# First shift and scale by halves of their columns, and four tiles of h contracted as soon as they are made

## What is computed

```python
mod = (jax.nn.silu(c) @ w_ada[i] + b_ada[i])[:, None, :]
shift_m, scale_m, gate_m, shift_f, scale_f, gate_f = jnp.split(mod, N_MOD, axis=-1)
h = rmsnorm(x, norm_mix_w[i]) * (1.0 + scale_m) + shift_m
x = x + gate_m * hybrid_mixer(h, w_in[i], ...)
...
proj = h @ w_in
z, xbc, dt_raw, u_pool, gate_logits = jnp.split(proj, IN_SPLITS, axis=-1)
xbc = jax.nn.silu(causal_depthwise_conv(xbc, conv_w, conv_b))
dt = jax.nn.softplus(dt_raw + dt_bias)
```

## Time and profile before

| | |
|---|---|
| time, median of 3 runs | 1705.75 us (1704.42 to 1709.04) |
| the profiled execution's own time | 1708.7 us |
| its span in the trace | 1706.9 us |
| PE busy | 1643.2 us, 96% of the span |
| chain that ended last | PE 80%, DVE 10%, ACT 4% |

### The profile page before, as it was taken

One profiled execution on the slowest core, in us unless ns is written; L12 is line 12 of the kernel. 1 busy time (PEld: TensorE's weight loads), 2 busy tenths in 40 slices (PEclk: granted clock), 3 DMA queues, 4 the chain that ended last, 5 costly groups with the idle time before them and its releaser, 6 DMA issues.

```text
span 1706.9 us, 21913 instructions
## 1 busy us (share of the span) xinstructions
PE 1643.2 (96%) x8026; PEld 1368.7 (80%) x8026; DVE 870.9 (51%) x1222; ACT 682.6 (40%) x1103; POOL 814.4 (48%) x670
## 2 busy tenths in 40 slices
PE   5988999999999999999999999989999999999997
PEld 5776888888878888888888889778878888888886
DVE  6546564656386435644335633677356655013324
ACT  3544445444323322543114322365646544234431
POOL 1373655636445554454444453432255454444443
PEclk7999999999999999999999999999999999999999
DMA  8121221222225445244545542121103142232221
GB/s 318 74 75 50 75 74 74 75 75 99 75 74 198 172 148 204 105 148 161 197 173 180 190 173 99 54 74 68 58 26 124 64 146 96 102 116 90 87 100 65
DMA packets 36825, 194.40 MB, mean 114 GB/s; under 512 B 4080, under 2 KB 6384, under 8 KB 21488
## 3 DMA queue, kind: packets, MB, share of 16 engines
q1 hardware_dynamic: 25200, 151.06, 24.4%
q10 hardware_dynamic: 11520, 41.95, 7.3%
HBM read 190.90 MB, written 2.10 MB: 113 GB/s over the span
## 4 chain that ended last, share of the span: by engine, by line
PE 80%; DVE 10%; ACT 4%; issue 2%; POOL 1%; DMA 1%; DVEq 0%; ACTq 0%; SPq 0%; POOLq 0%
PE main L900 59%; PE main L896 7%; PE main L893 2%; PE auxD L1211 2%; DVE tmp L2010 2%; ACT w_hi L1435 1%; PE main L1000 1%; DVE ada_first L2178 1%; DMA x<-x_in 1%; PE auxD L1276 1%; DVE ysum L2280 1%; PE auxC L1204 1%; PE auxB L1198 1%; DVE tmp L2575 1%; POOL w_lo L720 0%
## 5 line engine op out<-in xcount | busy, mean ns | idle before, releaser
L720 POOL TENSOR_TENSOR w_lo<-raw,w_hi 128x512 fp32r<-128x512 f32 x521 | 693.1, 1362 | 714.4 <-ACT w_hi L1435 710.8
L900 PE MATMUL main<-h_hi,w_hi 128*128 128x512 f32 (+1 forms) x1016 | 399.8, 394 | 1.0 <-DVEq L2077 1.0
L900 PE MATMUL main<-h_hi,w_lo 128*128 128x512 f32 (+1 forms) x1016 | 396.5, 390 | 0.0
L900 PE MATMUL main<-h_lo,w_hi 128*128 128x512 f32 (+1 forms) x1016 | 396.4, 390 | 0.0
L1435 ACT ACTIVATE w_hi<-raw 128x1024 fp32r<-128x1024 f32 (+2 forms) x267 | 258.2, 1015 | 249.1 <-PE main L900 175.2
L900 PEld LDWEIGHTS main<-h_hi,w_hi 128*128 128x128 f32 (+1 forms) x1016 | 190.9, 188 | 41.6 <-issue 2.1
L900 PEld LDWEIGHTS main<-h_hi,w_lo 128*128 128x128 f32 (+1 forms) x1016 | 190.7, 188 | 41.1
L900 PEld LDWEIGHTS main<-h_lo,w_hi 128*128 128x128 f32 (+1 forms) x1016 | 190.8, 188 | 39.4
L2153 DVE SCALAR_TENSOR_TENSOR tmp<-main,par,tmp 128x511 f32<-128x511 f32 x88 | 65.9, 749 | 161.8 <-ACT tmp L1547 160.0
L2178 DVE SCALAR_TENSOR_TENSOR ada_acc<-ada_raw,cs,ada_acc 128x1024 f32<-128x1024 f32 x70 | 106.3, 1519 | 35.0 <-DMA ada_raw<-w_ada 25.5
L2010 DVE SCALAR_TENSOR_TENSOR tmp<-main,half,tmp 128x511 f32<-128x511 f32 (+2 forms) x96 | 71.8, 748 | 44.5 <-ACT tmp L1456 42.1
(11 more groups left out here) (526 smaller groups left out, 2866.7 us busy)
## 6 DMA issues: line engine op xcount, KB each, us to landing
raw<-stream SPq DMA_DIRECT2D x118, 1024.0 KB, 4.8
ada_raw<-w_ada ACTq DMA_DIRECT2D x80, 512.0 KB, 4.5
ada_first<-w_ada SPq DMA_DIRECT2D x16, 512.0 KB, 10.2
raw<-stream SPq DMA_DIRECT2D x8, 768.0 KB, 4.2
raw<-stream SPq DMA_DIRECT2D x8, 640.0 KB, 3.9
x<-x_in SPq DMA_DIRECT2D x4, 512.0 KB, 8.2
x<-x_in SPq DMA_DIRECT2D x1, 2048.0 KB, 9.0
out<-x SPq DMA_DIRECT2D x16, 128.0 KB, 1.8
```

Source lines behind the costliest of these rows:

```text
L720: nc.gpsimd.tensor_tensor(lo[:, a:b], raw[:, s, a:b], hi[:, a:b], ALU.subtract).then_inc(lo_done, 1)
L900: ins = nc.tensor.matmul(bank[0:n, :], w[:, k, col:col + n], a[:, ka_, :], start=start, stop=stop)
```

## The change

- SP brings w_ada by halves of the columns, shift and scale in one DMA: 8 pieces of [128, 2, 512] for columns 0 to 511, then the raw weights of X0 and X1, then 8 pieces for columns 512 to 1023.
- The squares of x go to 8 buffers of their own and PE sums them over tiles and partitions (32 products with one column); DVE's adds go.
- ACT copies the spread 1/root to SBUF, POOL multiplies x by it (tiles 0 to 5 before X0's low pieces, 6 and 7 behind X1's). ACT makes the tile of h from it in two passes: scale and shift into `tmp`, then the rounded copy `h_hi`. `h_lo` becomes a plain subtraction on DVE.
- For the first half, PE takes 5 of the 16 products of w_ada pieces with silu(c) from DVE (`BY_PE`), 4 products with one column each.
- PE contracts DT, X0 and X1 together, over tiles 0 to 3 of h when these are there, then sums the second half of shift and scale, then contracts tiles 4 to 7. DT goes to bank A, so the four main banks hold X0's and X1's tiles, and later jobs are numbered one lower.
- X0 and X1 end together; their convolutions use buffers of their own (`conv_acc`), the tanh of one stands behind the scaling of the next, and `dt_gates`, `dt_sums` and group 0's `xs_turn` move to later slots.

The core of the diff:

```diff
@@ -122,7 +122,7 @@
+        job += 0 if x.name == "DT" else x.n_jobs
@@ -225,12 +225,13 @@
-    mid[find("X1")] += [("dt_turn", 0), ("dt_gates", 0)]
-    mid[find("BC")] += [("dt_sums", 0)]
+    mid[find("X1")] += [("dt_turn", 0)]
+    end[find("X1")] += [("dt_gates", 0)]
+    inner[find("BC"), 1] += [("dt_sums", 0)]
...
-            slot(2 * find("X1", g) + t).append(("xs_turn", (g, t)))
+            slot(2 * find("X1", g) + t if g else 2 * find("BC") + min(t, 2)).append(("xs_turn", (g, t)))
@@ -342,7 +343,7 @@
-    for stage in [("norm0", 0), ("ada_sum", 1), ("ada_sum", 0)] + order:
+    for stage in [("norm0", 0), ("ada_first", 0), ("dt_main", 0), ("ada_first", 1)] + order:
@@ -644,6 +645,23 @@
+        def early_tile(k):
+
+            return ada_raw[:, k // 2, SEQ * (k % 2):SEQ * (k % 2 + 1)]
+
+        def first_square(k):
+
+            return early_tile(k) if k < 4 else tmp[:, k - 4, :]
+
+        def conv_acc(cn):
+
+            if cn < 3:
+                return xdt[:, cn, :]
+            return y_part[:, :] if cn == 3 else tmp[:, cn % 2, :]
+
+        first_pieces = ada_first[:, :, :].rearrange("p (s k) c -> p s k c", s=2)
+        BY_PE = {0: ((1, 2), (0, 2), (1, 4), (0, 4), (0, 7)), 1: ()}
@@ -678,14 +696,16 @@
             load_unit(units[0])
-            for s in (1, 0):
+            for q in range(2):
+                cols = slice(SEQ * q, SEQ * (q + 1))
                 for k in range(KD):
-                    if s == 0:
+                    if q:
                         sp.wait_ge(first_in[k], 16)
-                    sp.dma_start(ada_first[:, KD * s + k, :],
-                                 w_ada[P * k:P * (k + 1), ADA_COLS * s:ADA_COLS * (s + 1)]).then_inc(first_in[k], 16)
-            load_unit(units[1])
-            load_unit(units[2])
+                    both = w_ada[P * k:P * (k + 1), 0:2 * ADA_COLS].rearrange("p (s c) -> p s c", s=2)
+                    sp.dma_start(first_pieces[:, :, k, cols], both[:, :, cols]).then_inc(first_in[k], 16)
+                if q == 0:
+                    load_unit(units[1])
+                    load_unit(units[2])
             for u in units:
                 if u.name == "OUT" and u.tag == 2:
@@ -812,7 +832,14 @@
+            def scale_first(k):
+
+                nc.gpsimd.tensor_tensor(x[:, k, :], x[:, k, :], rstd[:, :], ALU.mult).then_inc(add_first, 1)
+
             split_lo(units[0])
+            pool.wait_ge(aux_free["D"], 1)
+            for k in range(6):
+                scale_first(k)
             for u in units:
                 run(before[u.n])
@@ -821,6 +848,9 @@
+                if u.n == 1:
+                    scale_first(6)
+                    scale_first(7)
                 run(inner[u.n, 0])
                 run(early[u.n, 1])
@@ -1077,61 +1107,110 @@
...
+                def shift_and_scale(q):
+
+                    bank, full = take(("ada_first", q), 0)
+                    first = True
+                    for s, k in BY_PE[q]:
+                        pe.wait_ge(first_in[k], 16 * (q + 1))
+                        for t in range(4):
+                            nc.tensor.matmul(bank[:, 4 * s + t:4 * s + t + 1], ada_first[:, KD * s + k, chunk(4 * q + t)],
+                                             cs[:, 0, k:k + 1], start=first, stop=False)
+                            first = False
+                    pe.wait_ge(ada_ready, q + 1)
+                    for s in (1, 0):
+                        for t in range(4):
+                            ins = nc.tensor.matmul(bank[:, 4 * s + t:4 * s + t + 1], ada_first[:, KD * s, chunk(4 * q + t)],
+                                                   ones[:, 0:1], start=first, stop=(s == 0 and t == 3))
+                            first = False
+                    ins.then_inc(full, 1)
+
+                def dt_products(k):
+
+                    for a, w in ((h_hi, dt_hi), (h_hi, dt_lo), (h_lo, dt_hi)):
+                        if a is h_lo:
+                            pe.wait_ge(norm_lo, k + 1)
+                        ins = nc.tensor.matmul(dt_bank[0:HEADS, :], w[:, k, :], a[:, k, :], start=(k == 0 and a is h_hi and w is dt_hi),
+                                               stop=(k == KD - 1 and a is h_lo))
+                    return ins
+
+                def high(u, k):
+
+                    pe.wait_ge(hi_done, high_parts(u, (k + 1) * u.cols))
+                    for v, j, wh, wl in jobs:
+                        if v is u:
+                            nc.tensor.matmul(main[j][:, :], wh[:, k, :], h_hi[:, k, :], start=(k == 0), stop=False)
+                    pe.wait_ge(norm_lo, k + 1)
+                    for v, j, wh, wl in jobs:
+                        if v is u:
+                            nc.tensor.matmul(main[j][:, :], wh[:, k, :], h_lo[:, k, :], start=False, stop=False)
+
+                def low(u, k):
+
+                    pe.wait_ge(lo_done, low_pieces(u, k))
+                    for v, j, wh, wl in jobs:
+                        if v is u:
+                            nc.tensor.matmul(main[j][:, :], wl[:, k, :], h_hi[:, k, :], start=False, stop=False)
+
                 idle(16)
                 bank, full = take(("norm0", 0), 0)
-                pe.wait_ge(add_first, KD - 1)
-                for c in range(TC):
-                    ins = nc.tensor.matmul(bank[:, chunk(c)], rstd[:, chunk(c)], ones, start=True, stop=True)
+                for k in range(KD):
+                    pe.wait_ge(norm_sq, k + 1)
+                    for c in range(TC):
+                        ins = nc.tensor.matmul(bank[:, P * c:P * c + 1], first_square(k)[:, chunk(c)], ones[:, 0:1],
+                                               start=(k == 0 and c == 0), stop=(k == KD - 1 and c == TC - 1))
                 ins.then_inc(full, 1)
                 bank, full = take(("norm0", 0), 1)
                 pe.wait_ge(inv_first, 1)
                 for c in range(TC):
                     ins = nc.tensor.matmul(bank[:, chunk(c)], r_col[:, c:c + 1].to_broadcast([P, P]), ident, start=True, stop=True)
                 ins.then_inc(full, 1)
-                ada_sum(1, 0)
-                idle(20)
-                ada_sum(0, 1)
+                shift_and_scale(0)
                 idle(4)
-                for k in range(KD):
+                dt_bank, dt_full = take(("dt_main", 0), 0)
+                for k in range(4):
                     pe.wait_ge(norm_hi, k + 1)
...
+                    high(units[1], k)
+                    dt_products(k)
+                    low(units[1], k)
+                    high(units[2], k)
+                for k in range(4):
+                    low(units[2], k)
+                shift_and_scale(1)
+                for k in range(4, 6):
+                    pe.wait_ge(norm_hi, k + 1)
+                    for u in units[1:3]:
+                        high(u, k)
+                        low(u, k)
+                    dt_products(k)
+                pe.wait_ge(norm_hi, KD)
+                for k in range(6, KD):
+                    ins = dt_products(k)
+                ins.then_inc(dt_full, 1)
+                for u, j, wh, wl in jobs:
+                    for k in range(6, KD):
+                        for a, w in ((h_hi, wh), (h_lo, wh), (h_hi, wl)):
+                            ins = nc.tensor.matmul(main[j][:, :], w[:, k, :], a[:, k, :], start=False, stop=(k == KD - 1 and w is wl))
+                    ins.then_inc(main_full[j], 1)
 
...
+                def make(k):
+
+                    act.wait_ge(add_first, k + 1)
+                    act.wait_ge(mod_ready, 1 + k // 4)
+                    if k >= 4:
+                        act.wait_ge(norm_lo, k - 3)
+                    link(run_act(first_slot(k), x[:, k, :], ACT.Identity, scale=mul[:, 0, k:k + 1], bias=mod_at(0)[:, k:k + 1]))
+                    act.sem_inc(norm_tmp, 1)
+                    run_act(h_hi[:, k, :], first_slot(k), ACT.Copy).then_inc(norm_hi, 1)
+
+                split_hi(units[1], (0,))
+                make(0)
+                split_hi(units[1], (1,))
+                make(1)
+                split_hi(units[2], (0,))
+                make(2)
+                split_hi(units[2], (1,))
+                for k in range(3, KD):
+                    make(k)
@@ -1448,14 +1528,18 @@
             def convolve(u, t):
                 cn = conv_at[u.n, t]
                 w, b = conv_par(u, t)
-                if cn >= 2:
+                if cn == 4:
+                    finish_tanh()
+                if cn >= 4:
                     act.wait_ge(conv_s, cn - 1)
-                    if cn - 2 in turn_of:
-                        read_by_pe(turn_of[cn - 2], 0)
+                if cn >= 6 and cn - 2 in turn_of:
+                    read_by_pe(turn_of[cn - 2], 0)
                 bank, free = tile(u.job0 + t)
-                run_act(tmp[:, cn % 2, :], bank[:, :], ACT.Identity, bias=b, scale=w[:, 3:4]).then_inc(conv_a, 1)
```

(59 more changed lines are left out.)

137 lines of the change are left out of this document (39 added, 98 removed).

## The result

The changed kernel takes 1723.41 us (median of 4 runs, 1720.0 to 1725.75), the kernel before 1705.84 us beside it; the ratio is 1.0098, with a 95% interval of 1.0079 to 1.0117. It is slower by about 17 us (17.6 by the medians); I had forecast 1712 us, slower by 6 to 7, in a range up to 1719. The profiled execution took 1725.75 us, its span is 1724.0 us, and PE is busy for 96% of it as before. One execution of experiment 10 took 9374.68 us; its ratio leaves that one out, its median does not (1714.49 us without it).

What follows compares the result with a forecast made beforehand. PE, busy 96% of the span, bounds the kernel, waiting for DVE at the start. Z1's high parts end 6.7 us later (103.5 against 96.81): 1708.7 becomes 1715.4 profiled, less 2.95 for a median run: 1712 us, range 1701 to 1719.

Steps and rivals of the forecast that it cites:

- chain to the end of Z1's high parts: From X0's first result through convolutions, decays and weight splits to Z1's `w_hi`: 29.8 us, against 36.6 before.
- PE's second stall: PE standing for POOL behind Z1's high parts, at 110.72 before; to follow Z1's end unchanged, 6.7 us later.
- the 11.0 us for BC's two tiles: Term of the chain behind X0's first result: BC's two tiles with their turns and `dt_sums`, 11.0 us.
- six of the eight pieces begin only behind `h_lo` of tile 3, at 46.7: DVE's queue: second-half w_ada pieces stand behind the `first_low` steps, each waiting for ACT's tile; six begin at 46.7.
- a piece costs 1.32 x 1.5 = 2.0 until 52 and 1.35 after: DVE's second-half pieces: 2.0 us each beside POOL until 52, 1.35 after, so DVE is done at 56.5.
- the 1.12 of the earlier trace: DVE's `h_lo` beside POOL's pieces in the kernel before, 1.12 us, against 0.74 mostly outside them; basis for pricing pieces.
- 1 us of waits: PE's first half: waits for w_lo and h_lo, 1 us beside 15.1 us of products, ending at 54.8.
- Rival 4: DVE and POOL take strict turns, 1.27 + 0.67 apart; last pieces end at 60: 3.5 us more, 1716; chance 0.10.
- Rival 1: One-column products run at the high clock; first sums ready at 28, not 36.6: 1703.6 or 1700.6; chance 0.18.
- Rival 2: No PE bubble between the halves, DVE unhindered by POOL, pieces done at 54.6: 3 to 4 us less, 1709; chance 0.12.
- Rival 3: Chain behind X0 shorter than summed, `dt_gates` and splits slipping into ACT's waits: 5 to 9 us less, 1703 to 1707; chance 0.12.

Runs made afterwards that it cites:

- experiment 10: Changed kernel with one-column products made wide, x scaled by DVE out of PSUM, X0's products of tiles 4 to 7 ahead of X1's: 1714.82 us, 1.0047.
- experiment 1: Changed kernel with the first sums' one-column products writing 128 columns (squares) and 64 columns (shift and scale): 1721.51 us, 1.0089.
- experiment 7: Changed kernel without POOL's scaling of x and POOL's low pieces of X0 and X1 (one column of each kept): 1717.57 us, 1.0060.
- experiment 6: Changed kernel with DVE instead of POOL multiplying x by the spread 1/root, read in PSUM: 1723.04 us, 1.0092.
- experiment 11: experiment 10 plus four second-half half pieces on PE and the second sums ahead of three of X1's low steps: 1711.80 us, 1.0022.
- experiment 16: Kernel before with new convolution buffers and slots, squares on PE (128 columns), DVE's reciprocal two pieces later; repeat with more rounds: 1704.34 us, 0.9978.
- experiment 5: Changed kernel without POOL's multiplication of x by 1/root (only the first column of each tile scaled): 1722.44 us, 1.0096.

## Why the prediction was too low

| step | forecast | found |
|---|---|---|
| squares' products end; spread ends | 21.3; 24.1 | 22.5; 25.35 |
| one-column products of the first half end | 36.6 | 37.1 |
| first product with h (h_hi at 38.5) | 38.5 | 39.4 |
| h_lo of tile 3 done, last six pieces begin | 46.7 | 53.0 |
| these six take | 9.8 us | 8.65 us |
| PE through the first half | 54.8 | 57.8 |
| DVE's second half ready | 56.5 | 61.65 |
| sums of the second half | 2.8 us | 3.29 us |
| product with the fifth tile | 61.3 | 67.4 |
| X0's first result | 73.7 | 79.7 |
| chain to the end of Z1's high parts | 29.8 us | 31.9 us |
| Z1's high parts end | 103.5 | 111.6 |

- **Right.** That the one-column products run at 0.50 in the sums (experiment 1, with more columns in them, kept 1.00); that transfers are hidden; that X0's result falls behind X1's products (36 of X1's, 30 products more than before in all, 6.9 us, more than the first product had gained); that PE stands between the halves because DVE's pieces stand behind h_lo; that the chain gets shorter and that POOL and PE's second stall follow it. The sums hold within 0.2 us, but the 11.0 us for BC's two tiles in the chain rest on no row.
- **The step that failed** is "six of the eight pieces begin only behind `h_lo` of tile 3, at 46.7". This 46.7 is ACT's pace and one h_lo (ACT was done with tile 3 at 46.5, forecast 45.7); what POOL adds to DVE's h_lo and to the two pieces between them was put at nothing. Beside POOL three h_lo took 1.68, 1.66 and 1.63 us, the two pieces 2.96 and 3.48, and the six pieces began at 53.0. Counted from the first shift and scale, that is 15.9 us where the forecast had 10.1 (36.6 to 46.7), and 10.1 is what DVE takes when POOL makes next to nothing (experiment 7). The price that I did give the stretch, "a piece costs 1.32 x 1.5 = 2.0 until 52 and 1.35 after", was too low beside POOL (2.96 and 3.48 for the first two pieces) and was spent on the wrong ones: the six ran behind POOL and took 8.65 us, 1.1 less than forecast.
- **A row misread.** I took the 1.12 of the earlier trace rows for the price beside POOL and the 0.74 for one mostly outside it. But POOL works from 44.27 to 51.11, so the 0.74 (44.10 to 44.84) lies mostly beside it too; it had started 0.17 us ahead of POOL. And the 1.12 lies between what an h_lo takes free of POOL, 0.69, and the 1.66 found now. In the kernel before every second DVE instruction there reads PSUM; POOL may get on with its pass meanwhile and hold up the next h_lo for a part only. That reading fits the rows, but no run isolates it.
- **Its second price.** The same stretch made PE wait 2.5 us for low parts, where I had 1 us of waits; with the 0.9 of the start that is most of the 3 us by which the first half ended late. The fifth tile, 6.1 us late, is the sum: 0.5 from the first shift and scale, 5.8 from DVE's queue ahead of the six pieces, 1.1 less in them, and 1.0 because sums, mod and ACT took 5.8 us behind DVE and not 4.8. Everything from there to X0's result was right (12.3 us against 12.4).
- **Rival 4** named the kind of mechanism (DVE and POOL take turns) and I gave it 1 in 10 and 3.5 us. Its rule, from the Trainium skill, SBUF — State Buffer, section Who interferes with whom, agrees with the traces in which instructions are stretched: a DVE instruction with two SBUF inputs took 1.63 to 1.74 us beside POOL's passes of 1.47 to 1.71, and one with an input in PSUM was not stretched (0.61 in experiment 6). In size it does not: the rival's turn was 1.27 + 0.67 = 1.94 us, and from 41.76 to 53.00 DVE got one instruction through in 1.6 us on average (seven in 11.2). And the rival had only the last six pieces take turns, which were the ones that did not.
- **The rest.** The chain was 2.1 us longer than I summed, with two waits of ACT for DVE in it, 1.48 and 1.64 us, that I had taken for gone. Behind Z1, span less end of the high parts is 1612.4 us, against 1610.1 before; the same stretch with all but the same code is 1615.2 in experiment 11 and 1613.8 in experiment 16, so I can't put these 2.3 us down to the change. Of the 10.4 us by which the profiled execution was above the forecast (1725.75 against 1715.4), 6.0 come before X0's result, 2.1 in the chain and 2.3 behind it.
- **The other rivals.** Rival 1 fell with the clock at 0.50, and experiment 1 shows that even with the clock at 1.00 through the products with pieces it would not have come true: DVE was next, beside POOL. Rivals 2 and 3 fell with the gap and with the chain's length.

## What to carry to other kernels

When a step is moved, go through the queue of each engine it now runs beside, and price every instruction there, not only the moved ones, at the rate beside its new neighbour; a row whose mean lies between two clean values is a mixture and no price. Mending one engine of a front in which two or three are nearly tied can show nothing in the time (experiments 1, 5, 6): try the mendings together before calling one worthless. And part a change: here a chain part, worth 4.7 us of the chain inside the changed kernel, was bound to a merged front that put X0's first result 19.5 us later. But a part must be measured alone too: in the kernel before it shortened the chain by 3.4 us, and the time showed no gain.
